# A loop on the engines in place of 18 written-out iterations, with two steps of the chunk stage set elsewhere

## What is computed

```python
def _rwkv7_scan(s0, w, k, v, kk, a, r=None):
    def step(s, xt):
        wt, kt, vt, kkt, at = xt[:5]
        sa = jnp.einsum('bhvk,bhk->bhv', s, -kkt)
        s = (s * wt[:, :, None, :] + sa[..., None] * (kkt * at)[:, :, None, :]
             + vt[..., None] * kt[:, :, None, :])
        return s, jnp.einsum('bhvk,bhk->bhv', s, xt[5])

for d, f in enumerate((_ident, _flip)):      # both directions
    s_state, o = _rwkv7_scan(zero_rw, f(st_c['w'][d]), ...)   # 256 context tokens
    _, o = _rwkv7_scan(s_state, f(st_l['w'][d]), ...)         # 2048 latent tokens
```

## Time and profile before

| | |
|---|---|
| time, median of 3 runs | 4682.67 us (4679.31 to 4685.02) |
| the profiled execution | 4679.31 us, span 4677.4 us |
| instructions in the span | 74159 |
| busy share of PE, weight loads, DVE, ACT, POOL | 90%, 76%, 54%, 45%, 12% |
| granted TensorE clock, mean over the span | 0.948 |
| DMA of instructions (queues q8 and q14) | 4.03 MB of 688.70 MB |

### The profile page before, as it was taken

The page is one execution under the profiler, slowest core; times in us unless marked ns, Lnnn a source line. Parts: engine busy times, 40 slices in busy tenths (PEclk is TensorE's granted clock), DMA queues, the critical chain, the costliest instruction groups (busy, mean ns, idle before and its releaser), DMA issues. The chain is left out here.

```text
span 4677.4 us, 74159 instructions
## 1 busy us (share of the span) xinstructions
PE 4198.5 (90%) x29564; PEld 3555.5 (76%) x29600; DVE 2523.5 (54%) x3801; ACT 2104.8 (45%) x3194; POOL 550.2 (12%) x552
## 2 busy tenths in 40 slices
PE   7999999999699999999999696889739999999992
PEld 6878788888588888888888575668528888888881
DVE  5534435343377777677777496335454444444544
ACT  4434434333366666666666235113214444444443
POOL 1000000000211111111111033210000000000000
PEclk9999999999899999999999795899869999999996
DMA  6555554544322111112211336655346666566567
GB/s 238 186 192 177 181 167 155 160 154 151 99 58 57 50 51 51 51 53 60 56 50 51 111 107 191 221 187 170 107 161 218 216 206 214 211 219 209 214 215 269
DMA packets 384699, 688.70 MB, mean 147 GB/s; under 512 B 46669, under 2 KB 276277, under 8 KB 365465
## 3 DMA queue, kind: packets, MB, share of 16 engines
q1 hardware_dynamic: 360280, 591.20, 38.0%
q0 software_dynamic: 24128, 93.47, 6.6%
HBM read 539.15 MB, written 145.43 MB: 146 GB/s over the span
## 5 line engine op out<-in xcount | busy, mean ns | idle before, releaser
L106 PE MATMUL fro__acc<-fro__hT_hi,fro__wh 128*128 128x512 f32 (+1 forms) x1608 | 625.7, 389 | 7.4 <-DVE fro__hT_lo L2358 4.5
L108 PE MATMUL fro__acc<-fro__hT_lo,fro__wh 128*128 128x512 f32 (+1 forms) x1608 | 613.4, 381 | 0.0
L107 PE MATMUL fro__acc<-fro__hT_hi,fro__wl 128*128 128x512 f32 (+1 forms) x1608 | 613.3, 381 | 0.0
L1855 DVE TENSOR_TENSOR exp__wl<-exp__raw,exp__wh 128x4096 fp32r<-128x4096 f32 x97 | 429.2, 4424 | 331.3 <-ACT exp__wh L1807 331.3
L2364 DVE TENSOR_TENSOR fro__wl<-prj__w,fro__wh 128x1024 fp32r<-128x1024 f32 x201 | 246.2, 1225 | 645.7 <-ACT fro__wh L2168 645.7
L1807 ACT ACTIVATE exp__wh<-exp__raw 128x4096 fp32r<-128x4096 f32 x97 | 352.0, 3629 | 291.5 <-PE exp__acc L108 192.1
L106 PE MATMUL exp__acc<-exp__wh,exp__xh 128*128 128x512 f32 x1024 | 401.8, 392 | 2.6 <-DVE exp__xl L1860 2.6
L108 PE MATMUL exp__acc<-exp__wl,exp__xh 128*128 128x512 f32 x1024 | 399.4, 390 | 0.0
L107 PE MATMUL exp__acc<-exp__wh,exp__xl 128*128 128x512 f32 x1024 | 399.2, 390 | 0.0
L106 PEld LDWEIGHTS fro__acc<-fro__hT_hi,fro__wh 128*128 128x128 f32 x1608 | 304.0, 189 | 73.7 <-issue 18.0
L405 ACT ACTIVATE rwc__Tb<-rwc__TP 128x512 bf16<-128x512 f32 x432 | 234.2, 595 | 256.4 <-PE rwc__TP L763 256.4
(11 more groups left out here) (435 smaller groups left out, 8548.9 us busy)
## 6 DMA issues: line engine op xcount, KB each, us to landing
exp__raw<-in_w_x SPq DMA_DIRECT2D x98, 2048.0 KB, 8.3
prj__w<-in_w_z SPq DMA_DIRECT2D x201, 512.0 KB, 4.0
s_zT<-fro__zo SPq DMA_DIRECT2D x128, 256.0 KB, 4.4
fro__wm<-in_w_mod POOLq DMA_DIRECT2D x16, 1024.0 KB, 5.5
brp__gate<-s_zT SPq DMA_DIRECT2D x32, 512.0 KB, 4.7
rwc__kS<-s_kS SPq DMA_DIRECT2D x39, 256.0 KB, 3.0
rwc__kkn<-s_kkn SPq DMA_DIRECT2D x39, 256.0 KB, 3.4
rwc__kka<-s_kka SPq DMA_DIRECT2D x39, 256.0 KB, 4.2
```

The lines of the kernel that those rows point to most:

```text
L106: pe.matmul(out, sh, mh, start=first, stop=False)
L107: pe.matmul(out, sl, mh, start=False, stop=False)
L108: return pe.matmul(out, sh, ml, start=False, stop=last)
L1855: ve.tensor_tensor(wl[s][:, :, :], raw[s][:, :, :], wh[s][:, :, :], ALU.subtract).then_inc(w_lo, 1)
```

## The change

The 18 iterations become one loop that every engine runs (`Fori`). A count that depends on the iteration is now a register value, worked out by the sequencer ahead of its wait, and the addresses of SP's transfers come from registers (`snap`); SP also increments a semaphore `spent`, for which nothing waits, behind such waits. `decays` and `learning` are put together (`low_rank` on PE, `rates` on ACT) at the end of the body, so the learning rates are made one body earlier. `state` on DVE stands between the second and the third mask pair instead of behind the fourth. In the epilogue PE no longer waits for `bonc` and waits for the later count of `asg`.

```diff
@@ halves
-            for i in range(NT):
+            with eng.Fori(0, NT) as i:
                 for d in range(2):
-                    body(i, d, lambda name, k=0, ahead=0, h=2 * i + d: (h + ahead) * N[name] + k)
+                    body(i, d, lambda name, k=0, ahead=0, d=d: i * (2 * N[name]) + ((d + ahead) * N[name] + k))
@@ SP, body (soon and later in the same manner; sem_inc behind each further wait)
-                past = (NT + 2 - i) % NT * C if d == 0 else i * C
+                past = sp.snap(((i * -1 + (NT + 2)) % NT) * C if d == 0 else i * C)
                 sp.wait_ge(S["yc"], at("yc", 1) + START)
+                sp.sem_inc(spent, 1)
@@ ACT
-            def decays(d, at, ahead):
+            def rates(d, at, ahead):
                 act.wait_ge(S["um"], at("um", 1, ahead) + START)
                 act.wait_ge(S["dd2"], at("dd2", 0, ahead) + START)
                 act.activation(sg[:, :, :], f4(PB[0]), ACT.Sigmoid).then_inc(S["sgu"], 1)
-
-            def learning(d, at, ahead):
                 act.wait_ge(S["am"], at("am", 1, ahead) + START)
                 act.wait_ge(S["bd"], at("bd", 0, ahead) + START)
                 act.activation(av[:, :, :], f4(PB[1]), ACT.Sigmoid).then_inc(S["asg"], 1)
@@ ACT, body
                 copies(0, at)
-                learning(e, at, 1)
                 copies(1, at)
...
                 starts(e, at, 1)
-                decays(d, at, 2)
+                rates(d, at, 2)
@@ DVE
             def starts(d, at, ahead, state=None):
                 masked(0, d, at, ahead)
                 masked(1, d, at, ahead)
+                if state:
+                    state()
                 masked(2, d, at, ahead)
                 seeds(0, d, at, ahead)
                 masked(3, d, at, ahead)
-                if state:
-                    state()
                 seeds(1, d, at, ahead)
@@ PE, body
                 inverse_seed(at)
-                learning(e, at, 1)
                 couple(0, at)
...
                 turn(e, at, 1)
-                decays(d, at, 2, i + 1)
+                low_rank(d, at, 2, i + 1)
```

More of the change, by code:

```diff
@@ L270, in rwkv_chunks @@
         f4 = lambda b: b[:, :].rearrange("p (h c) -> p h c", h=4)
-        const_in, const_ok = sem("const_in"), sem("const_ok")
+        const_in, const_ok, spent = sem("const_in"), sem("const_ok"), sem("spent")
         lds = [sem(f"lds{d}") for d in range(2)]
@@ L325, in body @@
             def body(i, d, at):
-                past = (NT + 2 - i) % NT * C if d == 0 else i * C
-                soon = (NT + 1 - i) % NT * C if d == 0 else (i + 1) % NT * C
-                later = (NT - i) % NT * C if d == 0 else (i + 2) % NT * C
+                past = sp.snap(((i * -1 + (NT + 2)) % NT) * C if d == 0 else i * C)
+                soon = sp.snap(((i * -1 + (NT + 1)) % NT) * C if d == 0 else ((i + 1) % NT) * C)
+                later = sp.snap(((i * -1 + NT) % NT) * C if d == 0 else ((i + 2) % NT) * C)
                 sp.wait_ge(S["yc"], at("yc", 1) + START)
+                sp.sem_inc(spent, 1)
                 sp.dma_start(T["y"][1 - d, :, ds(past, C)].rearrange("(q p) t -> p q t", p=P), yo[:, :, :]).then_inc(y_out, 16)
@@ L464, in prologue @@
             def prologue(at):
-                decays(0, at, 0)
-                learning(0, at, 0)
+                rates(0, at, 0)
                 scale_bk(0, at, 0)
@@ L471, in prologue @@
                 starts(0, at, 0)
-                decays(1, at, 1)
+                rates(1, at, 1)
             def copies(l, at):
@@ L677, in _, with low_rank @@
             pe.wait_ge(const_ok, 4 + START)
-            def decays(d, at, ahead, i):
+            def low_rank(d, at, ahead, i):
                 pe.wait_ge(lds[d], i * (16 * NLD) + 16 * NLD + START)
@@ L731, in prologue @@
             def prologue(at):
-                decays(0, at, 0, 0)
-                learning(0, at, 0)
+                low_rank(0, at, 0, 0)
                 for q in range(4):
@@ L736, in prologue @@
                 turn(0, at, 0)
-                decays(1, at, 1, 0)
+                low_rank(1, at, 1, 0)
             def inverse_seed(at):
@@ L779, in right_side, with errors @@
                 m.then_inc(S["rhm"], 1)
-            def errors(g, e, at, ahead=1):
+            def errors(g, e, at):
                 if g == 0:
-                    pe.wait_ge(S["asg"], at("asg", 1, ahead) + START)
+                    pe.wait_ge(S["asg"], at("asg", 1, 1) + START)
                     pe.wait_ge(S["t32"], at("t32") + START)
@@ L861, in body @@
                 turn(e, at, 1)
-                decays(d, at, 2, i + 1)
+                low_rank(d, at, 2, i + 1)
             def epilogue(at):
                 right_side(1, at)
-                pe.wait_ge(S["bonc"], at("bonc", 1) + START)
-                errors(0, 1, at, 0)
-                errors(1, 1, at, 0)
+                errors(0, 1, at)
+                errors(1, 1, at)
                 outputs1(1, at)
```

## The result

The changed kernel took 4814.72 us (median of 4 runs, 4813.45 to 4814.91) against 4682.32 us for the kernel before (4 runs, 4679.31 to 4685.02): a ratio of 1.0283 (95% interval 1.0265 to 1.0300). The forecast was 4734 us with a range of 4700 to 4768. The direction was right, the size was not: 81 us are missing.

A forecast was written before the change was run, and what follows sets the result against it. It took a chain over PE, DVE and ACT at the change of passes as the bound. 0.83 + 0.49 + 0.1 = 1.42 us a pass, times 36 is 51 us: 4682.7 + 51 = 4734 us, range 4700 to 4768.

The forecast's parts named there:

- The state ahead of two mask pairs: On DVE, the state between mask pairs two and three delays the later masks and ACT's work: 0.83 us a pass.
- The learning rates ahead of the copies: On ACT, one more sigmoid between the decays' sigmoid and the `Tb` copies: 0.49 us a pass, bounds 0 and 0.62.
- the chain PE, DVE, ACT, PE at the change of passes: At the change of passes, DVE's fourth mask pair, through ACT's copies and sigmoid, holds PE's second half of `couple(0)`.
- Register work: Two sequencer operations behind the decisive wait at `right_side` on PE: 0.1 us a pass, bounds 0 and 0.5.
- The failed step: At PE's iteration end, 0.30 us of loop work, branch included, would lie under 1.05 us of products; no term added.
- The first rival: PE's loop too long to stay, first instructions fetched anew each branch: 16 to 31 us, 4750 to 4765 us; chance 0.20.
- the signs that were named for it: Passes alternating short and long, fetches at the old rate, gaps named "issue" on PE.
- The prediction's remark that 6.7 lines fit only near the head of a line: PE's loop of 6.7 lines fits 128 KB in 16 KB lines only if it starts near a line's head.

The follow-up runs named there:

- the shortened chain: Kernel before with the state in DVE's 0.86 us gap, both late masks ahead of the seeds, ACT's sigmoid table loaded early: 4650.5 us, ratio 0.9933.
- the changed kernel 200 later: Changed kernel with 200 instructions of satisfied waits more on PE ahead of its loop: 4738.7 us, ratio 1.0129.
- the changed kernel 100 later: Changed kernel with 100 instructions of satisfied waits more on PE ahead of its loop: 4862.2 us, ratio 1.0390.
- the kernel 24 later: Kernel before with the loop alone, old order of work, and 24 instructions of satisfied waits more on PE ahead of it: 4710.7 us, ratio 1.0080.

## Why the prediction missed, step by step

- **The state ahead of two mask pairs, 0.83 us a pass.** Right: 0.89 alone.
- **The learning rates ahead of the copies, 0.49.** Right: 0.49 alone. The two add up, so the chain PE, DVE, ACT, PE at the change of passes was read rightly; the shortened chain shows it from the other side. On the whole kernel the moves cost 46.2 us by the medians, 49.9 between the two profiled spans (4727.3 and 4677.4), where 36 x 1.38 is 49.7.
- **Register work, 0.1 a pass.** Mis-sized: with the loop alone the passes are 37.21 and 37.63 us in turn, 0.22 a pass over the 37.19 of the kernel before, and nearly all of it lies where an iteration ends, not in `right_side`. The 7.0 us by the medians agree with that, but that median may hold dear branches too: the profiled execution, which has none, lies 2.9 us above that of the kernel before.
- **The failed step: "At the end of an iteration PE has 32 + 208 + 59 ns = 0.30 us of loop work under 1.05 us of products".** It took the branch of the expert loop, 208 ns, for PE's branch in this loop, though it said itself that a loop of 6.7 packets is not shown, and the sum has no term for it. Here the branch is 4.43 us, outlasts the products and leaves PE at half clock. The cheap branch in the changed kernel 200 later, line numbers two higher:

```profile
1334.61 0.97 PEld L690 LDWEIGHTS rwc__PB<-rwc__aS,rwc__a 128*128 128x128 f32 x8 [0.85 <-ACT rwc__bo L408]
...
1335.49 0.32 PEld L743 LDWEIGHTS rwc__TP<-rwc__identb,rwc__TTb 128*128 128x128 bf16 x4
...
1337.49 0.23 PEld L752 LDWEIGHTS rwc__XB<-rwc__Tb,rwc__ATb 128*128 128x128 bf16 x4 [1.18 <-ACT rwc__Tb L408]
...
1340.89 0.32 PEld L761 LDWEIGHTS rwc__TP<-rwc__Xb,rwc__TTb 128*128 128x128 bf16 x4
```

  In the first iteration the seeds start 4.47 us later behind line 688 than in the kernel with the cheap branch (5.35 against 0.88 us); `double(0)` starts 11.99 us behind it against 6.28, 5.7 more, since PE's work up to there ran at half clock, less the 1.18 us for which PE waited there for `Tb` anyway. The pass is 44.70 us against 39.00, again 5.7. Over 17 branches it is 43.63 - 39.00 = 4.63 each, 79 us.
- **The first rival** had the right mechanism, 6.7 pieces against 5 shown, and the signs that were named for it came: short and long passes, "issue" on PE, and fetches, though not at the old rate but at 9 an iteration for 6.4. Its price was wrong. It took one fetch, by the landing of a 256 KB write, of which most would hide; in the trace the fetch behind the first branch goes out 2.4 us behind its start and takes 1.0 us, the branch ends 1.4 us behind that, and there is under 1 us of cover. It gave 0.9 to 1.7 us a branch; 4.6 was measured. It had no term at all for the clock. In the changed kernel 100 later, whose branches are only some 0.7 us longer, the granted clock is 0.50 until 1347, 11 us behind the branch's end at 1335.8, and a pass takes up to 48.8 us. The range, which ended at 4768, rested on that price.
- **The Trainium skill's sentence** in "Runtime: NRT & Kernel Launch", section "Instruction fetch mechanics", that a taken branch to code outside the window must fetch it first, was weighed against the expert loop and set aside "as a general rule". Both stand: the expert loop's code was there, this one's was not. The prediction's remark that 6.7 lines fit only near the head of a line does not follow from 128 KB in lines of 16 KB, which is eight of them; that the loop's place matters came true all the same.

The sum as measured: 4682 + 46 (moves) + 3 (the loop on the other four engines) + 79 (17 dear branches) = 4810. The missing 4 us, what is left of the 83.4 us of PE's loop, are its register work and its cheap share of the branch, by the difference alone.

## What to carry to other kernels

Compare the instruction fetches inside a loop with those of its first iteration: if a loop of PE runs close to what the engine holds, a hundred instructions ahead of it or the order of the work at its branch can decide a 2% change, and an experiment that shifts the code by a few hundred instructions tells this from any cause in the work itself. A step's price at a change of passes is read from the chain that ends last there; if it is right, the opposite edit gains what this one loses.

## What the runs showed of the hardware

- PE's compare-and-branch took 0.21 us where no fetch stood beside it and 3.5 to 6.3 us where the body was fetched anew. On the other four engines it took 0.04 to 0.07 us in all these loops.
- The same loop is cheap or dear by its place: 4738.7, 4814.7, 4828.4 and 4862.2 us for one kernel whose loop stands 200, 0, 248 and 100 instructions later (of the 4828.4, some 10 us are the added waits themselves).
- The times of one program with such a loop spread: 4682 to 4719 us for the loop alone, where the kernel before kept within 4679 to 4687. Its profiled run, 4682.2, had no dear branch; that the slower ones had some is likely by the kernel 24 later, but no trace of them shows it.
- PE, idle for 4.4 us, came back at a granted clock of 0.50 and had the full one some 5 us later.
- 100, 200 and 248 instructions of satisfied waits in one place moved the loop's start by only 0.8, 4.9 and 9.8 us (first register operation of the loop at 1253.0, 1257.1 and 1262.0 against 1252.2), where PE waits for its inputs anyway.
